# A streamed mixture-of-experts stage on one core: ten 2 MB weight slots, 16 KB rows, and the residual kept in PSUM

## What is computed

```python
h = rms_norm(x, norm_ffn_g) * (1.0 + scale2) + shift2
logits = h @ w_router + b_router                    # 32 experts, top 4 of each token
gates = softmax(top_val)
# for every expert e, over its tokens xb:
gu = xb @ w_gate_up[e] + b_gate_up[e]               # 1024 x 2048
gate, up = minimum(gu[:, :1024], 7), clip(gu[:, 1024:], -7, 7)
y = ((up + 1) * gate * sigmoid(1.702 * gate)) @ w_down[e] + b_down[e]     # 1024 x 1024
out[token] += y * gates
x = x + gate2 * out
return rms_norm(x, final_norm_g)
```

## Time and profile before

| | |
|---|---|
| runs, median of 3 | 1272.54 us (1272.43 to 1273.64) |
| the profiled execution | 1272.99 us, span 1271.0 us |
| mean granted TensorE clock | 0.986 |
| TensorE matmul / weight load | 1145.9 us (90%) / 534.4 us (42%) |
| VectorE / ScalarE / POOL | 406.3 us (32%) / 154.2 us (12%) / 19.3 us (2%) |
| DMA | 465.16 MB, mean 366 GB/s over the span |
| chain that ended last | PE 65%, DMA 28%, DVE 5%, ACT 1% |

### The profile page before, as it was taken

One profiled execution on the slowest core, in us unless ns is written; L12 is line 12 of the kernel. 1 busy time (PEld: TensorE's weight loads), 2 busy tenths in 40 slices (PEclk: granted clock), 3 DMA queues, 4 the chain that ended last, 5 costly groups with the idle time before them and its releaser, 6 DMA issues.

```text
span 1271.0 us, 14330 instructions
## 1 busy us (share of the span) xinstructions
PE 1145.9 (90%) x5357; PEld 534.4 (42%) x5357; DVE 406.3 (32%) x905; ACT 154.2 (12%) x277; POOL 19.3 (2%) x24
## 2 busy tenths in 40 slices
PE   3999999995999999999999998989899999999994
PEld 0588678854333333333333333333333333333332
DVE  3467236527513223131313131231313131313133
ACT  1111123501000010000000000001000000000003
POOL 1000000002000000000000000000000000000000
PEclk9999999996999999999999999999999999999998
DMA  9987931164899899999999999999999999999990
GB/s 345 372 342 304 392 153 67 67 269 198 333 424 424 351 422 426 422 428 420 426 424 424 425 422 426 423 423 424 426 422 427 420 426 422 426 425 422 424 392 34
DMA packets 66611, 465.16 MB, mean 366 GB/s; under 512 B 7434, under 2 KB 8060, under 8 KB 22524
## 3 DMA queue, kind: packets, MB, share of 16 engines
q1 hardware_dynamic: 63400, 460.98, 87.9%
q10 hardware_dynamic: 2788, 2.82, 0.8%
q0 software_dynamic: 400, 1.05, 0.3%
HBM read 463.79 MB, written 1.05 MB: 366 GB/s over the span
## 4 chain that ended last, share of the span: by engine, by line
PE 65%; DMA 28%; DVE 5%; ACT 1%; issue 1%; SPq 0%; ACTq 0%; DVEq 0%
DMA arena<-in_w_down 27%; PE ps L840 22%; PE ps L858 14%; PE ps L604 8%; PE ps L865 4%; PE ps L828 3%; PE ps L727 2%; PE ps L750 2%; PE ps L820 2%; PE ps L699 2%; PE ps L598 1%; PE ps L567 1%; PE ps L847 1%; DMA arena<-in_filt_freq 1%; PE ps L639 1%
## 5 line engine op out<-in xcount | busy, mean ns | idle before, releaser
L840 PE MATMUL ps<-arena 128*64 128x512 f32 x2048 | 444.9, 592 | 0.0
L840 PEld LDWEIGHTS ps<-arena 128*64 128x64 f32 x2048 | 148.1, 137 | 291.4 <-issue 291.4
L858 PE MATMUL ps<-arena 128*64 128x512 f32 x1024 | 229.2, 596 | 34.0 <-DMA arena<-in_w_down 33.4
L1467 DVE TENSOR_SCALAR arena<-ps 128x512 f32<-128x512 f32 x32 | 22.1, 691 | 475.5 <-PE ps L840 475.5
L858 PEld LDWEIGHTS ps<-arena 128*64 128x64 f32 x1024 | 72.4, 137 | 187.5 <-issue 163.1
L604 PE MATMUL ps<-arena 128*128 128x256 f32 x448 | 97.7, 379 | 0.0
L604 PEld LDWEIGHTS ps<-arena 128*128 128x128 f32 x448 | 84.9, 190 | 13.9 <-issue 2.6
L1505 DVE COPY arena<-ps 128x512 f32<-128x512 f32 x34 | 23.5, 692 | 202.8 <-PE ps L820 202.8
L1093 ACT ACTIVATE arena<-arena 128x512 f32<-128x512 f32 x32 | 20.1, 629 | 559.9 <-DVE arena L1467 559.9
L820 PE MATMUL ps<-arena 128*128 128x128 f32 x544 | 67.0, 283 | 22.5 <-ACT arena L1097 22.5
L820 PEld LDWEIGHTS ps<-arena 128*128 128x128 f32 x544 | 63.8, 196 | 26.6 <-issue 25.0
(11 more groups left out here) (245 smaller groups left out, 633.1 us busy)
## 6 DMA issues: line engine op xcount, KB each, us to landing
arena<-in_w_gate_up SPq DMA_DIRECT2D x256, 1024.0 KB, 19.0
arena<-in_w_down SPq DMA_DIRECT2D x64, 2048.0 KB, 14.6
arena<-in_w_ada SPq DMA_DIRECT2D x12, 2048.0 KB, 17.1
arena<-in_w_in SPq DMA_DIRECT2D x10, 2048.0 KB, 16.3
arena<-in_w_mix_out SPq DMA_DIRECT2D x2, 2048.0 KB, 8.9
arena<-in_w_hy_out SPq DMA_DIRECT2D x1, 2048.0 KB, 14.9
arena<-in_w_attn_out SPq DMA_DIRECT2D x1, 2048.0 KB, 19.3
arena<-in_x ACTq DMA_DIRECT2D x1, 1024.0 KB, 11.1
```

Of the source, the lines that this page charges most:

```text
L840: last = mm(ps[64 * h:64 * h + 64, 4 + b, :], hTp[:, k, s * 64:(s + 1) * 64], w[:, b * 1024 + h * 512:b * 1024 + (h + 1) * 512], start=Fal ...
L858: last = mm(ps[64 * h:64 * h + 64, 6, :], lhs, slots[c][:, qq, h * 512:(h + 1) * 512], start=(q == 0), stop=(q == 7))
```

## The change

What it does, part by part:

1. **Slots.** Ten of 2 MiB: four for the even item (`gu_a`, ring 0 to 3), four for the odd item (`gu_b`, over dft/inv/qm, over uc/kf, over ur, and over x/adr/on), two for down. `dynamic_dma_scratch_size=1024` and a new order of the regions make room for gate1, gate2 and the gate/up bias in regions of their own. The last slot lies over x.
2. **Rows.** w_gate_up is packed on the host as w_down was: a slot holds 256 input rows, 16 KB in one piece per partition.
3. **Order.** SP issues one order for each pair (`pair_of`): gate/up of the even item, down of the item before, gate/up of the odd item, down of the even item. The last down comes in four pieces of 1 MiB (8 KB per partition), behind the same queue.
4. **x1 in PSUM.** Four products with the identity put x1 into banks 0 to 3 before the ranks are made; the down bias, multiplied by gate2 on VectorE, is added to it.
5. **gate2.** Its copies to all partitions are made before the row squares. The copy of the down product to y moves from ScalarE to VectorE and multiplies by gate2. After the loop the banks hold x itself: ScalarE squares them in four halves, VectorE scales them straight into the output, SP stores four pieces.
6. **Gather.** `gather(p)` stands at the head of pair p, behind `place_weights`; the gather for a pair after the last is gone. The table of offsets is computed in bank 5 and copied between the halves of the first gather.
7. **Gate/up bias.** It lies on 64 partitions, 32 rows for each half of gate/up, in place of 128 partitions filled up with zeros; its products have 32 rows each.
8. **Small loads.** Nine loads of the front move from POOL's queue to ScalarE's, the two bias loads to ScalarE's and SP's.

```diff
-        gu_slot = [at("ring", 2048 * k, 2048) for k in range(KD)]
-        odd_slot = [span("ur", 2048, 2048), span("ur", 4096, 2048), span("ab", 0, 2048), span("dft", 0, 2048),
-                    span("qm", 0, 2048), span("ur", 0, 2048)]
+        NJ, NC = 4, 2
+        gu_a = ring[:NJ]
+        gu_b = [span("dft", 0, 4096), span("ur", 4096, 4096), span("ur", 0, 4096), span("x", 0, 4096)]
+        dn_row = ring[NJ:NJ + NC]
+        last_row = [at("ring", 2048 * c, 2048) for c in range(4)]
...
@@ SP @@
                 if blocks[last_use[f]] == ("mix", 0, 0):
+                    sp.wait_ge(S["s_ps"], 2 * HEADS)
+                    gate_up(gu_b[0], s_gub[0], 1, 0)
                     sp.wait_ge(S["pj_sb"], KD)
-                    gate_up(0, 1)
-                    gate_up(1, 1)
-                    sp.wait_ge(S["s_ps"], 2 * HEADS)
-                    gate_up(4, 1)
-                    sp.wait_ge(S["bc_sb"], 6)
-                    gate_up(2, 1)
+                    gate_up(gu_b[1], s_gub[1], 1, 1)
+                    sp.dma_start(b_down[0:E, :], a["b_down"][0]).then_inc(S["bd_in"], 16)
                 wait_used(blocks[last_use[f]])
...
+            sp.wait_ge(S["mix_ps"], 4)
+            gate_up(gu_b[2], s_gub[2], 1, 2)
+            sp.wait_ge(S["res_ps"], 1)
+            sp.wait_ge(S["xs_rdy"], TT)
+            sp.wait_ge(S["bc_sb"], 8)
+            gate_up(gu_b[3], s_gub[3], 1, 3)
+            def pair_of(p, e_a, e_prev, e_b):
+                for j in range(NJ):
+                    sp.wait_ge(S["gu_used"], p * 8 + (j - 7))
+                    gate_up(gu_a[j], s_gua[j], e_a, j)
+                for c in range(NC):
+                    sp.wait_ge(S["dn_used"], p * 4 + (c - 3))
+                    down(c, e_prev)
+                for j in range(NJ):
+                    sp.wait_ge(S["gu_used"], p * 8 + (j - 3))
+                    gate_up(gu_b[j], s_gub[j], e_b, j)
+                for c in range(NC):
+                    sp.wait_ge(S["dn_used"], p * 4 + (c - 1))
+                    down(c, e_a)
...
+            sp.wait_ge(S["gu_used"], q * 8 + 4)
+            for c in range(4):
+                sp.dma_start(last_row[c], w_dn[bass.ds(e_b, 1), c // 2, :, 2048 * (c % 2):2048 * (c % 2 + 1)]
+                             .rearrange("o p n -> p (o n)")).then_inc(s_gua[c], 16)
...
@@ TensorE @@
+            for t in range(TT):
+                for h in range(2):
+                    last = mm(bank(2 * t + h), ident, x[:, t, h * 512:(h + 1) * 512],
+                              start=True, stop=False, skip_group_check=True)
+            last.then_inc(S["res_ps"], 1)
             pe.wait_ge(S["m_rdy"], 1)
...
-                for b in range(2):
-                    for h in range(2):
-                        mm(ps[64 * h:64 * h + 64, 4 + b, :], mask[:, s, :],
-                           sel_bias[:, b * 1024 + h * 512:b * 1024 + (h + 1) * 512], start=True, stop=False)
+                for h in range(2):
+                    for b in range(2):
+                        mm(ps[64 * h:64 * h + 64, 4 + b, :], mask[E * b:E * b + E, s, :],
+                           sel_bias[E * b:E * b + E, h * 512:(h + 1) * 512], start=True, stop=False)
+                for j in range(NJ):
+                    w, landed = (gu_b[j], s_gub[j]) if s else (gu_a[j], s_gua[j])
+                    pe.wait_ge(landed, p * 16 + 16)
...
             with pe.Fori(1, n_pairs) as p:
+                pe.wait_ge(S["y_rdy"], p * 2 - 1)
+                pe.wait_ge(S["pt_sb"], p)
+                gather(p)
                 pe.wait_ge(S["mask_rdy"], p + 1)
...
                 pe.wait_ge(S["actT_rdy"], p * 2 + 2)
-                pe.wait_ge(S["y_rdy"], p * 2 + 1)
-                gather(p + 1)
                 pe.wait_ge(S["wt_rdy"], p + 1)
-                pe.wait_ge(S["ga_sb"], p * 2 + 3)
                 place_weights()
...
@@ ScalarE @@
+            for h in range(2):
+                every_partition(gate2B[:, 512 * h:512 * (h + 1)], 2, 2 + h)
...
-                    last = A(y[64 * s:64 * s + 64, 512 * h:512 * (h + 1)], ps[64 * h:64 * h + 64, 6, :], ACT.Copy)
...
+                for h in range(2):
+                    A(junk[:, 512 * (2 * t + h):512 * (2 * t + h + 1)], ps[:, 2 * t + h, :], ACT.Square,
+                      accum_out=ss4[:, 2 * t + h:2 * t + h + 1]).then_inc(S["fin_sq"], 1)
...
@@ VectorE @@
+            def y_copy(i, s):
+                v.wait_ge(S["dn_used"], i * 2 + 2)
+                for h in range(2):
+                    last = V.tensor_tensor(y[64 * s:64 * s + 64, 512 * h:512 * (h + 1)], ps[64 * h:64 * h + 64, 6, :],
+                                           gate2B[64 * h:64 * h + 64, 512 * h:512 * (h + 1)], ALU.mult)
+                last.then_inc(S["y_rdy"], 1)
...
             with v.Fori(1, n_pairs) as p:
                 st = Steps(v, S["dve_loop"], p * PER - PER)
+                gathered(p)
                 activate(p * 2, st)
+                y_copy(p * 2 - 1, 1)
                 v.wait_ge(S["pt_done"], p)
                 weigh(st)
...
                 activate(p * 2 + 1, st)
+                v.wait_ge(S["sc_done"], p)
+                y_copy(p * 2, 0)
                 rows_of(p + 1)
-                gathered(p + 1)
                 placed(p)
...
+                step(V.tensor_tensor(ss[:, t:t + 1], ss4[:, 2 * t:2 * t + 1], ss4[:, 2 * t + 1:2 * t + 2], ALU.add))
+                rstd(rs[:, t:t + 1], ss[:, t:t + 1], D)
                 for h in range(2):
-                    step(V.tensor_tensor(u_sb, ps[:, 2 * t + h, :], gate2B[:, 512 * h:512 * (h + 1)], ALU.mult))
-                    xs = x[:, t, 512 * h:512 * (h + 1)]
-                    sig(v, V.tensor_tensor(xs, xs, u_sb, ALU.add), "x2_rdy", 2 * t + h + 1)
...
+                    V.scalar_tensor_tensor(fin[:, t, 512 * h:512 * (h + 1)], ps[:, 2 * t + h, :], rs[:, t:t + 1],
+                                           fgB[:, 512 * h:512 * (h + 1)], ALU.mult, ALU.mult).then_inc(S["fin_rdy"], 1)
...
@@ host @@
+        if name == "w_gate_up":
+            v = v[0].reshape(E, 4, 2, P, 2 * FE).transpose(0, 1, 3, 2, 4).reshape(E, 4, P, 4 * FE)
```

More of the change, by code:

```diff
@@ L88, in host_tables @@
     put("lane", r[:, None])
+    put("lane32", r[:, None] % E)
     put("erev", E - np.arange(E)[None, :])
@@ L364, in _, with gate_up, down @@
                     sp.dma_start(dft, a["t_dft"].rearrange("(t p) f -> p t f", p=P)).then_inc(S["dft_in"], 16)
[L366 to L372, removed]
+            def gate_up(dst, landed, expert, j):
+                src = w_gu[expert, j] if isinstance(expert, int) else w_gu[bass.ds(expert, 1), j]\
+                    .rearrange("o p n -> p (o n)")
+                sp.dma_start(dst, src).then_inc(landed, 16)
+            def down(c, expert):
+                src = w_dn[expert, c] if isinstance(expert, int) else w_dn[bass.ds(expert, 1), c]\
+                    .rearrange("o p n -> p (o n)")
+                sp.dma_start(dn_row[c], src).then_inc(s_dn[c], 16)
             last_use = {n % 6: n for n in range(len(blocks))}
@@ L398, in _ @@
[L398 to L414, removed]
+                if f < NJ:
+                    gate_up(gu_a[f], s_gua[f], 0, f)
+                else:
+                    down(f - NJ, 0)
+            sp.wait_ge(S["mix_ps"], 4)
+            gate_up(gu_b[2], s_gub[2], 1, 2)
@@ L898, in _ @@
             pe.wait_ge(S["actT_rdy"], 1)
-            down(s_dn, dn_slot, 16)
+            down(s_dn, dn_row, 16)
             pe.wait_ge(S["act_rdy"], 2)
@@ L972, in _ @@
             act.dma_start(at("bv"), a["b_in"][0, 2560:3072].partition_broadcast(P)).then_inc(S["bv_in"], 16)
+            for b in range(2):
+                act.dma_start(sel_bias[E * b:E * b + E, :], a["b_gate_up"][0, :, D * b:D * (b + 1)]).then_inc(S["gub_in"], 16)
             act.dma_start(at("br"), a["b_router"][0].partition_broadcast(P)).then_inc(S["br_in"], 16)
@@ L1097, in act_copy @@
                 A(actT.rearrange("p j s -> p (j s)"), ps[:, 7, :], ACT.Copy).then_inc(S["actT_rdy"], 1)
-            def y_copy(i, s):
-                act.wait_ge(S["dn_used"], i * 2 + 2)
-                for h in range(2):
-                    last = A(y[64 * s:64 * s + 64, 512 * h:512 * (h + 1)], ps[64 * h:64 * h + 64, 6, :], ACT.Copy)
-                last.then_inc(S["y_rdy"], 1)
             act.wait_ge(S["gt_ps"], 1)
@@ L1504, in gathered @@
                     v.wait_ge(S["ga_done"], p * 2 + (half + 1))
+                    if half and isinstance(p, int):
+                        v.wait_ge(S["ex_ps"], 1)
+                        step(V.tensor_copy(exc, ps[:, 5, 384:432]))
                     V.tensor_copy(hTp[:, 4 * half:4 * half + 4, :].rearrange("p k s -> p (k s)"), ps[:, 7 - half, :])\
```

214 lines of the change are left out of this document (77 added, 137 removed).

## The result

The changed kernel takes 1253.59 us (median of 4 runs, 1252.26 to 1254.92); the kernel before took 1272.76 beside it (4 runs, 1272.43 to 1273.64). The ratio is 0.985, interval 0.983 to 0.987: faster by 19 us, where 36 were forecast, and 1.6 us above the upper end of the range. The profiled execution took 1254.92 us with a span of 1253.1; 1234.8 had been forecast for the span.

The account below looks back on a forecast made before the run. The prediction took the DMA weight stream as the bound: 22 us from its rate, 3 from the tail, some 13 from the last down product's lag, less 2 for the hole, taking 1272.54 to 1236.3 us; range 1230 to 1252.

Parts of the forecast that it names:

- term 1: Weight stream: 16 KB gate/up rows run at 435 GB/s, 8 KB at 420; a pair takes 57.9 us instead of 59.35.
- about 1255: Result if the skill's packet overhead held: an 8 KB row loses 1.2%, a 16 KB row 0.6%.
- Term 2: Start of the unbroken stream: DMA stands still about 15 us from 343; item 1's w_down is issued at 356.8.
- Each saves 0 to 0.9: Two gate/up bias blocks of 1.9 us, now 32-row products on two row groups: each gains 0 to 0.9 us.
- they may bring the clock back earlier: 0 to 3 us: New x1 products in TensorE's idle stretch before the ranks may restore its clock sooner, worth 0 to 3 us.
- Its eight instructions end at 1219.6: End of the stream: last w_down piece lands at 1217.8 and its down product ends at 1219.6.
- The short hole: Near 386.3 the stream waits for item 1's half before w_down of item 2: 1.2 us with the restart.
- Term 3: TensorE's clock per pair: 54.8 to 56.7 us, middle 55.8, so the stream stays the bound by a narrow margin.
- rival B: Gap after the down product grows and TensorE is the bound, from 56.8 us a pair; 1246.2 us at 57.5; chance 0.10.
- Term 4: Tail from the last down product to the end of the span: 15.2 us, before 18.2.
- C: Slower than before: gather waits lengthen each pair, from 59.4 us a pair; 1281 us at 60; chance 0.04.
- A: Row length does nothing to the weight stream, rate stays at 424 GB/s: 1258.4 us; chance 0.13.

Follow-up runs that it names:

- experiment 1: Changed kernel with w_gate_up back in 8 KB rows, slots, DMA size and order kept: 1263.58 us, ratio 0.991 to the kernel before.
- experiment 4: Changed kernel with every second gate/up and down product left out, all weights still loaded: 1239.63 us (one execution).
- experiment 7: Changed kernel with pairs 1 to 3 asked for in the order slots come free, back to the loop's order in pair 4: 1240.09 us.
- experiment 9: Changed kernel with the slot-free order in early pairs, its return spread over pairs 4 to 6, one gate/up piece per step: 1238.17 us.
- experiment 6: Changed kernel with item 3's gate/up before item 1's w_down, in pair 1 only: 1251.84 us, ratio 0.981 to the kernel before.

## Why the prediction was half right

**The step that failed is the size of term 1: "I take 435 and 420."** The bound, its place and the sign were right: late pairs have a DMA share of 1.01, and experiments 1 and 4 show that the stream's packets and nothing else set them. But 16 KB rows run at 428.4 and 8 KB rows at 422. On 352 MiB, 2.4475 us per MiB instead of 2.41 is 13.2 us, less 0.1 on the last 4 MiB: 13.1 of the 18.3 that the span was off. I had chosen the pair (435, 420) from two windows of the earlier trace rows and the mean of 424; but the mean is met by (428.4, 422) as well, so the split came from the windows alone, and both were misread. The row taken for w_down alone begins while 8 KB rows still run: of its packets 42 are of 8 KB and 219 of 16 KB. And a packet counts whole in the window in which it starts: at the prices measured above these packets are 42 x 0.3106 + 219 x 0.612 = 147 us of work, and 16 engines have 144 in 9 us. Without the surplus 437 is 428; the row's DMA share, 1.03 beside 1.01 over a pair, is the sign of it. Both windows of the kernel before once more, moved by 1 us, so that each holds one kind of row (but for a packet):

```profile
978.60:987.60 9.00, 9.00 (x43) 3.02 (x44) 0.00 (x0) 1.26 (x3) 0.00 (x0) 1.00 1.00 426
989.00:1021.00 32.00, 30.02 (x150) 12.58 (x148) 4.62 (x8) 2.42 (x4) 0.00 (x0) 1.00 1.01 422
```

In a steady stream such a window errs both ways: twelve of 9 us end to end from 700 on in the changed kernel, all in 16 KB rows, read 424 to 433 where the pairs show 428 and 429; the third and the fourth:

```profile
718.00:727.00 9.00, 9.00 (x44) 3.01 (x42) 2.77 (x4) 0.63 (x1) 0.00 (x0) 1.00 1.00 424
727.00:736.00 9.00, 8.42 (x44) 2.60 (x42) 6.30 (x17) 0.60 (x1) 0.00 (x0) 1.00 1.02 433
```

By the Trainium skill ("DMA: Bandwidth & Descriptors", Where 436 GB/s comes from) the ports into SBUF allow 435.2 GB/s. The trace agrees: the bytes' share of the packet times above is 435, and no pair shows more than 429. A row of 437 lay above that ceiling, and this should have told me that the window over-reads. Of the Trainium skill's rule on the cost of a packet ("DMA: Bandwidth & Descriptors", Why small descriptors are slow), which the prediction weighed as "about 1255", the runs bear out the direction and not the size: it has some 3 beats of 32 bytes, and 0.0094 us measured is 8 beats at 0.602 us for 512. That put the true gain, 1.5% between 8 and 16 KB, between the 0.6% of that rule and my 3.6%, nearer to the former.

**Term 2, the hole.** Right in place, length and cause: a DMA share of 0.11 from 343 to 358, and SP waiting for the first half of item 0's down product. The issue came at 358.67 instead of 356.8, +1.9, which is less than the front differs between executions. That the hole was a loss was priced at a net of 2 us; by the account above it is about 4. What was mis-sized is what it was netted against: I took 8 us for the later holes of the kernel before, and the one at 433 is 6 x (1.01 - 0.21) = 4.8:

```profile
433.00:439.00 6.00, 6.00 (x30) 2.01 (x28) 0.09 (x1) 0.00 (x0) 0.00 (x0) 1.00 0.21 59
```

The 14.3 idle now, less 4.8 and less 4.9 for the 2 MiB fetched ahead, are 4.6. Having netted it, I did not ask what it was worth to be without it; experiments 7 and 9 show that it was worth 11 and 14 us to an order of issue that avoids it, since every microsecond that the stream stands still in a kernel bound by it comes back at the end. "Each saves 0 to 0.9" for the bias block came out at 0.85 (1.94 to 1.09), and "they may bring the clock back earlier: 0 to 3 us" at nothing: first gather 5.57 us after 5.67.

**The end of the stream, a step that I didn't price.** "Its eight instructions end at 1219.6" put the last down product 1.8 us behind the landing of the last piece. That piece is issued at 1202.8 and lands 31.5 us later, at 1234.3, and the product ended 4.1 us behind it. When the last gate/up piece has landed at 1214.6, TensorE still has 3.65 + 3.64 + 7.02 + 2.36 + 7.11 = 23.8 us to do, and the stream only 8 MiB, 19.6 us. So the last two items are TensorE's again, some 2.3 us over what I wrote. With 13.1 and 1.9, 17.3 of the 18.8 us by which that product was late are named. The short hole that I had priced at 1.2 near 386 did not come (no 4 us between 380 and 396 have a DMA share under 0.98), so 2.7 stay open; the restart after the long hole is 0.8 of them (a share of 0.85 in 360 to 365).

**Term 3** was right within its bounds. Gather 2.41 us behind the down product (2.35 forecast), bias 7.03 (6.95), TensorE's pair 55.0 in 54.8 to 56.7, and at the low end, since the bias block does gain from running on two row groups. The Trainium skill's rule ("TensorEngine Tiling (Array Packing)", Key Properties: tiles operate independently) gave 54.8, and the trace agrees with it: eight products of 32 rows in 1.09 us where eight of 128 took 1.94. So TensorE's bound lies further off than the middle I took, and rival B has no ground.

**Term 4**, the tail: 14.7 against 15.2.

**The rivals.** B is out (55.0 against 56.8 from which it decides), C too (no pair over 58.8). A, row length worth nothing, is refuted by experiment 1 by 8.5 us, but its figure of 1258.4 was closer than mine: the truth lay between the two cases, and a continuous size had been treated as two cases with a gap between them, 1241 to 1258. The range ended in that gap.

## What to carry to other kernels

A rate that decides a sum is to be read over whole periods, and compared over periods of different mixes; a stretch of a few microseconds can read 1 to 2% high or low, as much as the effect that is looked for. In a kernel bound by its stream, price the idle time of the stream first and ask what head of the issuing queue makes it: here the order in which slots come free, left again in small steps, was worth 14 us, 16 KB rows 8.5. And when a stream ends, compare what the consumer still has to do after each late piece with what is left of the stream.

## What the runs showed that was not expected

- A packet costs 0.0094 us on its DMA engine beside its bytes: 24 MiB in 16, 8 and 4 KB rows take 58.74, 59.64 and 61.44 us (428, 422 and 410 GB/s). Whether 1 or 2 MiB are moved by one DMA makes no difference in a full queue (59.35 and 59.34 us).
- A return from one order of issue to the other costs some 3 us in one jump, whether in pair 4 or 5 (883.1 to 884.0 against 880.4), and next to nothing in small steps.
- The front differs between executions by some 5 us. Sixteen products took 4.75 us in the changed kernel's profile, in a window with a granted clock of 0.83 (rows below), where the kernel before took 3.46 at 1.00; and T0 came at 354.5 in experiment 6 and 354.1 in experiment 7, whose front is the changed kernel's. No edit explains it; it is why spans were compared from T0 on.

The chain of waits of the changed kernel near 227 us, and its window 222 to 232:

```profile
227.33 4.75 PE ps L661 x16
```

```profile
222.00:232.00 10.00, 8.00 (x33) 6.57 (x32) 5.20 (x17) 1.20 (x4) 0.00 (x0) 0.83 0.00 0
```

- The second gate/up block lasts 15.06 us at 340 in the changed kernel and 13.88 elsewhere, with a granted clock of 0.75 in 340 to 345; without the x1 products it is the same (15.25). The kernel before has 1.00 there. TensorE is busy all of 335 to 345 in both, and what lowers the clock stays open.
